# Modulation vectors from split weights, two tiles a turn, beside the scaling of the activations

## The reference

```python
s_lat = silu(c); s_ctx = silu(c_ctx)                     # two vectors of 2048
m_lat = split(s_lat @ w_mod + b_mod, 6)                  # shift, scale, gate, ...
m_ctx = split(s_ctx @ w_mod + b_mod, 6)
hx = rmsnorm(x,   norm_mix) * (1 + m_lat[1]) + m_lat[0]
hc = rmsnorm(ctx, norm_mix) * (1 + m_ctx[1]) + m_ctx[0]
... = split_cols(hx @ w_in), split_cols(hc @ w_in)       # three token mixers: LRU, attention, short convolution
```

## Time and profile before

| | |
|---|---|
| median of three runs | 3165.56 us (3165.32 to 3170.72) |
| profiled execution, its own time | 3173.48 us |
| its span, first to last instruction | 3171.7 us |
| busy share of the span | PE 85%, PEld 59%, DVE 61%, ACT 30%, POOL 19% |
| mean DMA rate | 286 GB/s |
| chain that ended last | PE 48%, DMA 28%, DVE 10%, issue 9%, ACT 3% |

### The profile page before, as it was taken

The page is one execution under the profiler, slowest core; times in us unless marked ns, Lnnn a source line. Parts: engine busy times, 40 slices in busy tenths (PEclk is TensorE's granted clock), DMA queues, the critical chain, the costliest instruction groups (busy, mean ns, idle before and its releaser), DMA issues.

```text
span 3171.7 us, 33622 instructions
## 1 busy us (share of the span) xinstructions
PE 2708.2 (85%) x11665; PEld 1856.2 (59%) x11665; DVE 1949.5 (61%) x2602; ACT 936.7 (30%) x1257; POOL 598.8 (19%) x580
## 2 busy tenths in 40 slices
PE   8899997998887999999999636968778778788778
PEld 3488775878675889999878513434334334343323
DVE  2389996433766777888555566555556565655652
ACT  1167775431454443333443200101111111111100
POOL 0000000000000000000000153534343434443341
PEclk9999998999999999999999868999989899999999
DMA  8633334542211877888556499999999999999996
GB/s 325 225 122 117 108 117 146 192 152 80 94 68 64 345 307 290 342 318 319 199 200 244 178 388 412 416 421 409 422 409 422 399 422 409 421 399 422 421 421 272
DMA packets 126334, 906.72 MB, mean 286 GB/s; under 512 B 13984, under 2 KB 15264, under 8 KB 16416
## 3 DMA queue, kind: packets, MB, share of 16 engines
q0 software_dynamic: 82944, 604.02, 46.4%
q1 hardware_dynamic: 38304, 278.94, 23.7%
q10 hardware_dynamic: 4992, 22.65, 1.8%
HBM read 901.33 MB, written 4.23 MB: 286 GB/s over the span
## 4 chain that ended last, share of the span: by engine, by line
PE 48%; DMA 28%; DVE 10%; issue 9%; ACT 3%; POOL 1%; DVEq 0%; ACTq 0%; POOLq 0%
DMA u<-in_peer_u,idx 27%; PE ps L424 12%; PE ps L467 6%; PE ps L468 6%; PE ps L469 6%; PE ps L760 6%; PE ps L482 3%; PE ps L439 2%; DVE u L1619 2%; PE ps L642 1%; DVE wl L1134 1%; PE ps L624 1%; DVE ub L1218 1%; POOL v L1692 1%; DVE tt L1229 1%
## 5 line engine op out<-in xcount | busy, mean ns | idle before, releaser
L760 PE MATMUL ps<-v,dg 128*128 128x512 f32 x2048 | 929.2, 610 | 199.1 <-DMA v<-in_peer_v,idx 100.0
L1619 DVE SCALAR_TENSOR_TENSOR u<-u,hN 128x2048 f32<-128x2048 f32 x256 | 586.5, 2292 | 486.8 <-DMA u<-in_peer_u,idx 474.9
L760 PEld LDWEIGHTS ps<-v,dg 128*128 128x128 f32 x2048 | 391.3, 195 | 732.7 <-issue 571.6
L1134 DVE TENSOR_TENSOR wl<-w,wh 128x1024 fp32r<-128x1024 f32 x432 | 525.1, 1222 | 373.9 <-ACT wh L805 373.1
L805 ACT ACTIVATE wh<-w 128x1024 fp32r<-128x1024 f32 x432 | 453.2, 1058 | 731.9 <-PE ps L469 317.7
L424 PE MATMUL ps<-both,wh 128*128 128x256 f32 x2560 | 475.6, 288 | 5.4 <-DVE y L1343 5.1
L1685 POOL DMA_INDIRECT u<-in_peer_u,idx x256 | 281.8, 1101 | 886.7 <-DVE u L1619 459.6
L424 PEld LDWEIGHTS ps<-both,wh 128*128 128x128 f32 x2560 | 404.6, 194 | 17.1 <-issue 15.0
L424 PE MATMUL ps<-both,wl 128*128 128x256 f32 x1280 | 363.5, 284 | 0.0
L1090 ACT ACTIVATE dg<-con,wt 128x128 f32<-128x128 f32 x256 | 99.1, 399 | 852.2 <-PE ps L760 846.9
L1692 POOL DMA_INDIRECT v<-in_peer_v,idx x256 | 282.7, 1104 | 188.4 <-PE ps L760 104.8
(11 more groups left out here) (229 smaller groups left out, 2920.3 us busy)
## 6 DMA issues: line engine op xcount, KB each, us to landing
w<-in_stream SPq DMA_DIRECT2D x264, 1024.0 KB, 4.8
mr<-in_wmod POOLq DMA_DIRECT2D x64, 1024.0 KB, 6.7
wg<-in_gates ACTq DMA_DIRECT2D x8, 512.0 KB, 3.4
u<-in_peer_u,idx POOLq DMA_INDIRECT x256
v<-in_peer_v,idx POOLq DMA_INDIRECT x256, 18.0
xs<-in_ctx ACTq DMA_DIRECT2D x1, 2048.0 KB, 17.0
xs<-in_x ACTq DMA_DIRECT2D x1, 2048.0 KB, 22.6
x<-in_x ACTq DMA_DIRECT2D x1, 2048.0 KB, 7.5
```

Of the source, the lines that this page charges most:

```text
L760: last = mm(ps[:, b, :], dg[:, k % 4, :], V[n % NV][:, b * 512:(b + 1) * 512], start=(k == 0), stop=(k == TOPK - 1))
L1134: tt(wl[p % SPLITS][:, :, :], W[s][:, q * PIECE:(q + 1) * PIECE, :], wh[p % SPLITS][:, :, :].bitcast(F32), ALU.subtract)\
L1619: stt(U[n % NU][:, :], U[n % NU][:, :], 1.0, hN[:, t, :], ALU.mult, ALU.mult, accum_out=dot[:, t, k:k + 1])\
```

## The change

The 32 halves of the modulation are reordered so that a turn of four halves brings 256 columns of shift and the same 256 columns of scale, two tiles of 128 channels. Halves 0 to 2 of a turn are split like other weights, six pieces a turn (`MP` = 6), numbered m = 6c + p; the fourth half stays plain fp32 with `sT`. The stationary operand of the split pieces is `sS`, 4 columns (high and low of the two vectors) for `wh`, 2 columns for `wl`. So a turn has 48 fp32r matmuls of 256 columns and 8 plain ones. Behind each turn DVE copies 4 rows (2x256 columns) to `mrow`; PE turns them to columns (`rows_turn`) in the middle of the next turn, DVE makes shift and scale of the two tiles from them (`mod_cols`), and in a later turn ACT makes both the high part and the scaled value of these two tiles (`tiles`, 8 instructions) and DVE the low part (`tile_lows`, 4). DVE no longer scales the tiles. The transposes of `xs` come after three turns instead of four, and every second tile of `xT` is copied by ACT. SP frees slots 0 to 2 by `mod_lo` (DVE's low parts), slot 3 by PE.

```diff
+            def mod_turn(c):
+                b = 2 * (c % 2)
+                if c >= 2:
+                    pe.wait_ge(rows_copied, 2 * (c - 1))
+                for p in range(MP):
+                    m = MP * c + p
+                    pe.wait_ge(mod_lo, m + 1)
+                    for kk in range(PIECE):
+                        k = p % 4 * PIECE + kk
+                        mm(ps[0:4, b + p // 4, 0:CW], sS[:, k, 0:4], wh[m % SPLITS][:, kk, :], start=(k == 0), stop=False, skip_group_check=True)
+                        last = mm(ps[0:2, b + p // 4, 0:CW], sS[:, k, 0:2], wl[m % SPLITS][:, kk, :], start=False,
+                                  stop=(k == KT - 1), skip_group_check=True)
+                    last.then_inc(piece_used, 1)
+                    if p == 2 and c >= 3:
+                        rows_turn(c - 1)
+                pe.wait_ge(arrived[RING - 1], 16 * (c + 1))
+                for kk in range(HK):
+                    last = mm(ps[0:2, b + 1, 0:CW], sT[:, HK + kk, :], W[RING - 1][:, kk, :], start=False, stop=(kk == HK - 1), skip_group_check=True)
+                last.then_inc(piece_used, 2)
+            def rows_turn(c):
+                pe.wait_ge(rows_copied, 2 * (c + 1))
+                if c:
+                    pe.wait_ge(*VM.at(c - 1, "s0"))
+                for i in range(4):
+                    last = nc.tensor.transpose(ps[:, 4, 4 * i:4 * i + 4], mrow[0:4, c % 2, i * P:(i + 1) * P], ident[0:4, 0:4])
+                last.then_inc(rows_turned, 1)
...
+            for c in range(3):
+                mod_turn(c)
...
+            rows_turn(0)
+            rows_turn(1)
+            for c in range(3, MODS):
+                mod_turn(c)
+            first_piece(0)
+            rows_turn(MODS - 1)
+            for p in range(1, 4):
+                first_piece(p)
...
+            def mod_split(m):
+                c, p = divmod(m, MP)
+                act.wait_ge(arrived[p // 2], 16 * (c + 1))
+                if m >= SPLITS:
+                    act.wait_ge(piece_used, 8 * ((m - SPLITS) // MP) + (m - SPLITS) % MP + 1)
+                fn(wh[m % SPLITS][:, :, :], W[p // 2][:, p % 2 * PIECE:(p % 2 + 1) * PIECE, :], ACT.Copy).then_inc(mod_hi, 1)
+            def tiles(c):
+                act.wait_ge(*VM.at(c, "s1"))
+                for k in (2 * c, 2 * c + 1):
+                    for w, to, at, v in SIDES:
+                        x, scale, bias = xT[:, k, at:at + T], mcol[:, KT + k, v:v + 1], mcol[:, k, v:v + 1]
+                        fn(to[0][:, k, :], x, ACT.Identity, scale=scale, bias=bias).then_inc(*AH.inc("h" + w))
+                        act.wait_ge(*AH.at(k, "h" + w))
+                        fn(x, x, ACT.Identity, scale=scale, bias=bias).then_inc(*AH.inc("v" + w))
+            for m in range(4):
+                mod_split(m)
             act.wait_ge(xs_in, 32)
             for i in range(4):
...
+                mod_split(4 + 2 * i)
+                mod_split(5 + 2 * i)
...
+            for c in range(3, MODS):
+                for p in range(3):
+                    mod_split(MP * c + p)
+                for i in {3: (0,), 4: (1, 2)}.get(c, (c - 2,)):
+                    tiles(i)
+                for p in range(3, 6):
+                    mod_split(MP * c + p)
+            tiles(MODS - 2)
+            split(LRU0, 0, 0, 0)
...
+            tiles(MODS - 1)
+            split(LRU0, 0, 0, 3)
...
+            def mod_rows(c):
+                if c >= 2:
+                    dve.wait_ge(rows_turned, c - 1)
+                for b in (0, 1):
+                    dve.wait_ge(piece_used, 8 * c + (8 if b else 4))
+                    nc.vector.tensor_copy(mrow[0:4, c % 2, b * CW:(b + 1) * CW], ps[0:4, 2 * (c % 2) + b, 0:CW]).then_inc(rows_copied, 1)
...
             for i in range(4):
                 tsc(xs[:, i, :], xs[:, i, :], rin0[:, i:i + 1], None, ALU.mult).then_inc(*V0_.inc(f"xn{i}"))
+                mod_low(2 * MP + i)
+            mod_rows(1)
...
+            for c in range(3, MODS):
+                for p in range(4):
+                    mod_low(MP * c + p)
+                mod_cols(c - 1)
+                for p in range(4, 6):
+                    mod_low(MP * c + p)
+                for i in {3: (0,), 4: (1, 2)}.get(c, (c - 2,)):
+                    tile_lows(i)
+                mod_rows(c)
+            low(LRU0, 0, 0, 0)
+            tile_lows(MODS - 2)
+            mod_cols(MODS - 1)
+            low(LRU0, 0, 0, 1)
+            low(LRU0, 0, 0, 2)
+            tile_lows(MODS - 1)
+            low(LRU0, 0, 0, 3)
```

More of the change, by code:

```diff
@@ L470, in wide @@
                     last.then_inc(piece_used, 1)
[L472 to L482, removed]
-                            last.then_inc(piece_used, 2)
@@ new lines, in rows_turn, with first_piece @@
+            def rows_turn(c):
[5 more added lines that the diff above has]
+                last.then_inc(rows_turned, 1)
+            def first_piece(p):
+                pe.wait_ge(*VH.at((p + 1) * PIECE - 1, "lo_x"))
+                proj_both(LRU0, 0, 0, 0, part=(p,))
@@ L496, in _ @@
                 last.then_inc(*P0.inc(f"xT{k}"))
-            mod_turns(MOD_H // 8, MOD_H // 4)
-            pe.wait_ge(*VM.at(MOD_H // 4 - 1, "m1"))
-            for i in range(2 * KT):
-                last = nc.tensor.transpose(ps[:, 2, 2 * i:2 * i + 2], mrow[0:2, i * P:(i + 1) * P], ident[0:2, 0:2])
-            last.then_inc(*PM.inc("rows"))
-            for p in range(4):
-                pe.wait_ge(*VH.at(0, f"lo_x{(p + 1) * PIECE - 1}"))
-                proj_both(LRU0, 0, 0, 0, part=(p,))
+            pe.wait_ge(xt_copied[0], KT // 2)
+            rows_turn(0)
[6 more added lines that the diff above has]
+                first_piece(p)
             def lru_turn(j, more):
@@ L795, in _ @@
                 fn(junk[:, :], xs[:, i, :], ACT.Square, accum_out=ssq[:, i:i + 1]).then_inc(*A0.inc(f"ss{i}"))
+                mod_split(4 + 2 * i)
+                mod_split(5 + 2 * i)
+                if i == 0:
+                    act.wait_ge(*V0_.at(0, "abs"))
+                    fn(lm[2][:, :], lm[1][:, :], ACT.Exp, scale=-1.0).then_inc(*A0.inc("ez"))
             act.wait_ge(*A0.at(0, "ss3"))
@@ L798, in _ @@
             fn(rin0[:, :], ssq[:, :], ACT.Sqrt, scale=1.0 / D, bias=tiny[:, 1:2]).then_inc(*A0.inc("rt"))
+            for m in range(12, 3 * MP):
+                mod_split(m)
+            for k in range(1, KT, 2):
+                act.wait_ge(*P0.at(0, f"xT{k}"))
+                fn(xT[:, k, :], ps[:, 4 + k % 4, :], ACT.Copy).then_inc(xt_copied[1], 1)
             def split(first, turn, per, p, slots=None):
@@ L805, in split @@
                 fn(wh[p % SPLITS][:, :, :], W[s][:, q * PIECE:(q + 1) * PIECE, :], ACT.Copy).then_inc(hi_done, 1)
-            for k in range(KT):
-                for w, to, at in (("c", hc, 0), ("x", hx, T)):
-                    act.wait_ge(*VH.at(0, f"{w}{k}"))
-                    if k % PIECE == 0 and w == "c":
-                        split(LRU0, 0, 0, k // PIECE)
-                    fn(to[0][:, k, :], xT[:, k, at:at + T], ACT.Copy).then_inc(*AH.inc(f"{w}{k}"))
+            for c in range(3, MODS):
[7 more added lines that the diff above has]
+            split(LRU0, 0, 0, 0)
+            split(LRU0, 0, 0, 1)
+            split(LRU0, 0, 0, 2)
+            tiles(MODS - 1)
+            split(LRU0, 0, 0, 3)
             act.wait_ge(*VZ.at(0, "lru"))
@@ L1145, in _ @@
+            for m in range(MP):
+                mod_low(m)
             lam = pc("lam", 0, 2 * KT)
@@ L1169, in _ @@
             tsc(cof[:, 1, :], lm[5][:, :], -8.0, None, ALU.mult).then_inc(*V0_.inc("c8"))
+            mod_rows(0)
+            for m in range(MP, 2 * MP):
+                mod_low(m)
             dve.wait_ge(*A0.at(0, "rt"))
```

119 lines of the change are left out of this document (64 added, 55 removed).

## The result

The changed kernel took 3174.18 us (median of 16 runs, 3170.17 to 3176.84) against 3167.82 of the kernel before on the same chip: ratio 1.0016, interval 1.0009 to 1.0024. That is 2.9 to 7.6 us slower, 5.1 in the middle. The middle lies inside the 6.3 us (0.2%) of the forecast, in their upper part; the upper end of the interval lies beyond them, and so, just, does the plain difference of the two medians, 6.4. The profiled execution took 3174.63 with a span of 3172.8; granted clock 0.939, before 0.945.

A forecast was written before the change was run, and what follows sets the result against it. TensorE bounded the kernel; changed, DVE and TensorE alternate. Modulation end 143.4 plus tail 26.1 is 169.5, plus 6 for the clock 175.5 against 173.33: 2.2 us later, 3167.8, no change within 6.3 us (chance 0.58); range 3155 to 3184.

The forecast's parts named there:

- x lands: Start: the transfer of x lands at 28 us, bounds 25.6 and 28.1, with weight loads taking part of its rate.
- first low part of turn 3: End of the start: DVE begins turn 3's first low part at 76.3 us, 5.4 earlier but one turn fewer done.
- turn 3, turn 4: Modulation: turn 3 takes 14.2 us, ACT's fourth split 1.2 late; turn 4 takes 14.7, with two pairs of tiles.
- turns 5 to 7: Steady modulation turns: 12.9 us each against 13.84 before, 38.7 for three; ACT's work and the loads hidden in it.
- modulation ends (copy): DVE's last row copy of the modulation at 143.4 us, against 137.24 before.
- tail, without the clock: Modulation's end to the end of the first four LRU projection pieces: 26.1 us at 2.4 GHz, against 36.1 before.
- mark without the clock: End of L439's run, the first four LRU projection pieces: 169.5 us at 2.4 GHz throughout, against 173.33 before.
- the clock: TensorE's clock falling after gaps: turn heads 3.5 us, tail about 1.5, turn 2 1; sum 6, bounds 0 and 15.
- mark: End of L439's run, the first four LRU projection pieces: 175.5 us against 173.33 before, a shift going through to the end.
- the doubt between 0.12 and 0.43: Time of one narrow 256-column fp32r matmul on TensorE in us: 0.12 taken, 0.43 kept as an outer end.
- the turn as a hand-over between DVE and TensorE alone: Steady turn: 8.5 us of DVE's copy, low parts and columns, then TensorE's last piece 0.96 and plain half 3.46.
- The rival with a fast loop: Modulation: DVE's copy doesn't hold back the next turn; turns of 9.5 or 10.0 us, 15 to 17 less, 3151; chance 0.06.

The follow-up runs named there:

- experiment 6: Changed kernel plus useless plain matmuls in TensorE's waits (turn 2, ahead of turn 3, turn 4, tail): 3172.48 us, ratio 1.0005 to the kernel before.
- Experiment 3: Changed kernel with ACT's two tile steps as plain copies, scale and shift left out: 3166.84 us, ratio 0.9993 to the kernel before.
- experiment 1: Changed kernel with DVE's row copies moved behind the next turn's first two low parts: 3172.12 us, ratio 1.0007 to the kernel before.
- experiment 5: Kernel of experiment 1 with ACT's tiles behind a turn's six splits, DVE's tile low parts one turn later: 3169.70 us, ratio 0.9999 to the kernel before.
- experiment 2: Changed kernel with ACT making pieces 4 to 7 and the exponential before waiting for x: 3166.33 us, ratio 0.9992 to the kernel before.
- experiment 9: Kernel of experiment 8 with the first two pairs of tiles both scaled in turn 3: 3147.22 us, ratio 0.9928 to the kernel before.
- experiment 7: Changed kernel with two blocks split, two plain and first, eight splits before x's wait, tiles behind the splits: 3157.56 us, ratio 0.9961 to the kernel before.
- experiment 4: Changed kernel with all four weight blocks plain fp32, no splits, tiles still scaled beside the modulation: 3157.99 us, ratio 0.9968 to the kernel before.
- experiment 8: Kernel of experiment 7 with a turn's weight transfers issued in slot order 0, 2, 1, 3: 3152.22 us, ratio 0.9947 to the kernel before.

## Why the prediction came out as it did

The forecast was no change, with 2.2 us later; the ratio says 5.1 (2.9 to 7.6). Step by step:

| step | forecast | measured |
|---|---|---|
| x lands | 28 | 28.8 |
| first low part of turn 3 | 76.3 | 76.46 |
| turn 3, turn 4 | 14.2, 14.7 | 15.1, 17.6 |
| turns 5 to 7 | 12.9 each | 13.0, 12.95, 13.7 |
| modulation ends (copy) | 143.4 | 148.4 |
| tail, without the clock | 26.1 | 26.3 (27.9 less 1.6) |
| mark without the clock | 169.5 | 173.6 (experiment 6) |
| the clock | 6 | 2.7 |
| mark | 175.5 | 176.28 |

- **Right:** narrow fp32r matmuls cost 0.117, so the doubt between 0.12 and 0.43 is settled; the start up to turn 3, the tail's order, and above all that a turn (5 and 6) would save 1 us and not 4, though TensorE has only 9.5 us of work in it.
- **Mis-sized, the scaled tiles:** "a pair of tiles costs 3.2", bounds 2.6 and 4. It is 4.5. I had taken a copy (L813, 0.33 in a row, 0.8 for two that wait) for an operation with a scale and a bias per partition. Experiment 3, which runs about my price, ends at 169.20 where the sum without the clock said 169.5: this one term carries the miss of the modulation's end. It doesn't carry turn 3, which is 0.9 over the forecast at either price (why isn't shown), and turn 4 I had 1.7 too long at mine.
- **Mis-sized, the clock:** 6 forecast, 2.7 shown by filling the waits. I had given each head of a turn an even chance of a fall, from the 1.83 us gap in the earlier trace rows. The same gap, 1.73, at the heads of turns 4 to 7 and ahead of the first LRU piece, brought none. The other falls that I had named (turn 2, the tail) came and cost about what I said. The Trainium skill, "TensorE: Matmul & The Clock Gate", section "A second HAM failure mode: psum-queue depth-cycling", warned of short repeated idles; this trace doesn't bear it out in turns 5 to 7, with 1.00 granted from 104 to 148, and does in turn 2, where waits of 0.90, 1.25 and 0.69 us between pieces were followed by 0.62. What tells 1.73 here from 1.83 in the attention stage isn't settled by these runs.
- The two misses have opposite signs, +4.1 and -3.3; that the mark came out within 0.8 us is partly luck.
- **Failed, part of the reason for 12.9:** the turn as a hand-over between DVE and TensorE alone. The sum met the measured 12.95, and each copy does wait 3.07 for L499, but taking that loop away moved no turn from 5 on by more than 0.4, and these three together grew by 0.3 (experiment 1). "ACT (6 x 1.05 + 3.2 = 9.5) is hidden in it. The loads are too" was the false step, with "is not read before the next": ACT comes to the next turn's slot 0 about 5 us into the turn (113.98), when its transfer has only been issued (111.53). With 4.5 for tiles ACT has 10.8 us of work, and it waits 1.9 to 3.1 us more for slot 0 and 0.5 to 1.8 for slot 1. In experiment 1 that wait is made by the one queue, where slot 3 stands ahead of slot 0; in the changed kernel by DVE's low parts, which free slot 0 only behind the copy. With the copies moved and the tiles put where ACT waited, the modulation ended 6.8 us earlier (experiment 5).
- **Not seen at all:** ACT's 12.44 idle us ahead of x. I had read off that pieces 4 and 5 stand behind that wait and priced it, but not what it is worth to undo: 7.5 us (experiment 2), more than the whole change moved.
- The rival with a fast loop (3151, chance 0.06) was rightly small for this kernel; its time is passed by experiment 9 with two split blocks, but by turns of 12.1 and an earlier start, not by its turns of 10.

## What to carry to other kernels

When work is taken off the busy engine and given to two others, write down for each a whole turn in its order of issue, transfers among them, and look for every loop of about the same length; opening one of two gained 0.9 us here. Try the parts of a change singly: here one part was worth -8.7 us and the other +11.7 on top of it. Two split blocks in place of three, with the plain ones and the tiles placed as in experiment 7, beat three with the same early start (experiment 2), were level with none (experiment 4), and beat none only once the transfers and tiles were reordered (experiment 9); what the number of blocks does alone wasn't run. And in a queue that issues in order, order the transfers by when their slots come free, not by slot number (6.7 us at the mark, experiment 8).

## What the runs showed of the hardware that I had not expected

- ACT's activation with a scale and a bias per partition takes 586 and 601 ns for 128x256, the copy of the same tile 401 and 417.
- Gaps of 1.73 us on TensorE in turns of 13 left the granted clock at 1.00; it fell behind 4.29 (to 0.57) and in turn 2, behind waits of 0.90, 1.25 and 0.69 us between pieces of 0.96 (0.62 over 60 to 64). One or two matmuls in each of these waits of turn 2 kept it at 1.00 there (experiment 6). The length of a gap alone doesn't tell: in the tail it fell behind 1.94 in the changed kernel and behind 1.75 in experiment 4, and stayed at 1.00 behind 1.95 in experiment 3.
- A 2 MB transfer took 22.6, 23.3, 23.5 or 25.8 us from issue to landing, the longer the earlier the second round of weight transfers began (issued from 19.30 in the kernel before, 18.99 in experiment 4, 18.55 in experiment 7, 15.96 in the changed kernel).
